# One kernel's expert gelu taken one chunk later, and TensorE's wait moved from the gelu to the sum

## The chip, the cores and the metric

The kernel runs on one core of a Trainium2 chip. The metric is the device time of one execution in microseconds (us). The core's engines work side by side and meet only at semaphores: TensorE (PE; its weight loads are PEld), VectorE (DVE), ScalarE (ACT), GpSimd (POOL) and SyncE (SP), whose queue issues most DMAs.

## The reference

A decoder layer for 256 tokens of width 2048, float32: an input projection, a gated delta rule and a retention beside each other, an output projection, then the part that matters here, and a gated embedding with a last norm. The part that matters is a mixer of 16384 one-neuron experts:

```python
q = (xt @ w_pq).reshape(t, PK_HEADS, 2, PK_DQ // 2)
scores = jnp.einsum('thpc,hpnc->thpn', q, sub_keys)
s1, i1 = lax.top_k(scores[:, :, 0], 16); s2, i2 = lax.top_k(scores[:, :, 1], 16)
# 16 best of the 256 sums per token and head: idx, gates = softmax
pre = jnp.einsum('tkd,td->tk', expert_u[i_blk], x_blk)
act = jax.nn.gelu(pre, approximate=False) * g_blk
out = jnp.einsum('tk,tkd->td', act, expert_v[i_blk])
```

The kernel does not gather. It computes `pre` for all 128 x 128 experts and all tokens, applies the gelu, multiplies by a map of gates that is zero where an expert was not chosen, and multiplies by all of expert_v.

## The kernel before, in words

**Tiles.** All large weights come as one stream of tiles of 128 x 1024 float32 (512 KB). SP loads tile n into one of four `raw` buffers. ScalarE rounds it to `hi` (`round_tile`, L208 to L213), VectorE takes the rest `lo = raw - hi` (`rest_tile`, L215 to L220), TensorE multiplies by both (`pair_tile`, L229 to L242): 8 products of hi with both halves of the activations (512 columns, L236), then 8 of lo with one half (256 columns, L240). There are two `hi` and two `lo` buffers. So round n waits until TensorE is through with hi of tile n-2 (`hi_used`) and VectorE has taken the rest of tile n-2 (`lo_ready`); rest n waits for round n and until TensorE is through with lo of tile n-2 (`lo_used`).

**Expert chunks.** The stage has 128 chunks of 128 experts, two tiles each (T_U on), 256 tiles. Chunk c is accumulated in PSUM bank 6 + c % 2. Its two halves are summed by VectorE into `pre[:, c % 2]` (`take_pre`, L1134 to L1136, one tensor_reduce), which stands in VectorE's queue behind the rest of the second tile of chunk c+1. ScalarE's gelu (`gelu_chunk`, L733 to L735) reads `pre` and writes chunk c to SBUF. In ScalarE's queue the order is: the two rounds of chunk c, then the gelu of chunk c-1 (`expert_round`, L737 to L742). The gelu adds one to `expert_bank`, which starts at 2; TensorE waits for `expert_bank >= c + 1` before chunk c (L1617), that is for the gelu of chunk c-2.

**What VectorE does beside it.** For the first 144 tiles VectorE also chooses the experts. A unit (`choose`, L1138 to L1201) is one head of one block of 128 tokens: eight tiles, and between them the top-16 searches, in an order written out by hand. There are 16 units. After every fourth comes `weigh` (L1211 to L1230): a subtraction of the largest score (L1215, raises `gates_in`), an exp on ScalarE (L751, between expert rounds, it needs another activation table), four plain tiles, and the sums and products of the gates (L1224 to L1230), which raise `gates_ready`. POOL then scatters the gates to a map in HBM, 64 scatters for each `weigh` (L1396). The remaining 112 tiles run without choosing (`plain`, L1203).

**Behind the stage.** SP waits until all 256 scatters have landed (L523), loads the first two blocks of the map (L515), and goes on with the tiles of expert_v. ScalarE's `value_round` (L756) and VectorE's `gated_block` (L1255) begin the next stage; the last gelu and the last sum stand in their first tiles (L768, L1259).

Of the kernel before, what the change touches and what calls it, by code (L numbers as in the profile page):

```python
# [75 lines left out]
CHUNKS = N_KEYS  # L76
# [48 lines left out]
def build(nc, x, w_in_cols, w_in_rows, w_ab, w_out, w_pq, expert_u, expert_v, w_gate, w_ple, p_t,  # L125
          positions, keep_c, mix_c, norm_cols, conv_cols, sub_keys_t, ab_cols, dn_norm, ret_gn_w,
          ret_gn_b, norm_final, out, h_spill, gate_map):
    with ExitStack() as ctx:
# [3 lines left out]
        def sem(name):  # L132
            return ctx.enter_context(nc.semaphore(name))
# [63 lines left out]
        def hold(eng, name, s, value):  # L197

            eng.wait_ge(s, value)
            eng.sem_inc(held[name], 1)  # L200
# [7 lines left out]
        def round_tile(act, n, slot, use, turn, first=False):  # L208
            act.wait_ge(weights_landed[slot], 16 * turn + 16)
            if not first:  # L210
                act.wait_ge(hi_used, n - SPLIT + 1)
                act.wait_ge(lo_ready, n - SPLIT + 1)
            act.activation(hi[:, use, :], raw[:, slot, :], ACT.Copy).then_inc(hi_ready, 1)  # L213
# [8 lines left out]
        def tile_at(base, i, per, k):  # L222

            assert base % RAW == 0 and per % RAW == 0
            return (base + k + per * i, (base + k) % RAW, (base + k) % SPLIT,
                    (base + k) // RAW + (per // RAW) * i)
# [17 lines left out]
        def both_halves(bank):  # L244
            return ps[:, bank, :].rearrange("p (h t) -> p t h", h=2)
# [93 lines left out]
        def wait_turned(pe, turn, d, banks):  # L339
# [93 lines left out]
        expert_bank, gates_in, gates_exp, gates_ready = (sem("expert_bank"), sem("gates_in"), sem("gates_exp"),  # L433
                                                         sem("gates_ready"))
        pre_ready, zeros_ready, map_cleared, gates_placed = sem("pre_ready"), sem("zeros_ready"), sem("map_cleared"), sem("gates_placed")
# [52 lines left out]
        def _(sp):  # L488
# [8 lines left out]
            def stream(base, source, start, stop):  # L497

                with sp.Fori(start, stop) as i:
                    for k in range(RAW):  # L500
                        n, slot, _, _ = tile_at(base, i, RAW, k)
                        load_tile(sp, n, slot, source[ds(i * RAW + k, 1)].rearrange("a p f -> (a p) f"))
# [15 lines left out]
            def value_block(j):  # L518
                for k in range(RAW):
                    n, slot, _, _ = tile_at(T_V, j, RAW, k)  # L520
                    load_tile(sp, n, slot, expert_v[ds(j * RAW + k, 1)].rearrange("a p f -> (a p) f"))
# [21 lines left out]
        def _(act):  # L543
# [189 lines left out]
            def gelu_chunk(c, parity):  # L733
                hold(act, "act", pre_ready, c + 1)
                act.activation(experts[:, ds(c, 1), :], pre[:, parity:parity + 1, :], ACT.Gelu).then_inc(expert_bank, 1)  # L735

            def expert_round(i, first=False):  # L737
                for c in range(2):
                    for k in range(2):
                        round_tile(act, *tile_at(T_U, i, 4, 2 * c + k))  # L740
                    if not (first and c == 0):
                        gelu_chunk(2 * i + c - 1, 1 - c)  # L742

            expert_round(0, first=True)
            for w in range(WEIGHINGS):
                with act.Fori(max(1, WEIGH_ROUNDS * w), WEIGH_ROUNDS * (w + 1) - 1) as i:
                    expert_round(i)

                units = slice(WEIGH_UNITS * w, WEIGH_UNITS * (w + 1))
                act.wait_ge(gates_in, w + 1)  # L750
                act.activation(gates3[:, units], gates3[:, units], ACT.Exp).then_inc(gates_exp, 1)  # L751
                expert_round(WEIGH_ROUNDS * (w + 1) - 1)
# [3 lines left out]
            def value_round(half, i, late=0, first=False):  # L756

                if half == 0:
                    hold(act, "act", gated, i + 1)
                for c in range(4):  # L760
                    v = CHUNKS * half + 4 * i + c
                    if not (first and c < 2):
                        hold(act, "act", lo_used, T_V + v + late - 1)
                    act.activation(stage_hi[:, c % 2:c % 2 + 1, :], experts[:, ds(4 * i + c, 1), :],  # L764
                                   ACT.Copy).then_inc(stage_hi_ready, 1)
                    round_tile(act, T_V + v + late, c % RAW, c % SPLIT, (T_V + late) // RAW + CHUNKS // RAW * half + i)
                    if first and c == 0:
                        gelu_chunk(CHUNKS - 1, 1)  # L768

            value_round(0, 0, first=True)  # L770
            with act.Fori(1, CHUNKS // 4) as i:
                value_round(0, i)
            with act.Fori(0, CHUNKS // 8) as i:
                value_round(1, i)
# [42 lines left out]
        def _(dve):  # L817
# [315 lines left out]

            def take_pre(c, parity):  # L1134
                dve.wait_ge(lo_used, T_U + 2 * c + 2)
                dve.tensor_reduce(pre[:, parity, :], both_halves(U_BANK + parity), AX_X, ALU.add).then_inc(pre_ready, 1)  # L1136

            def choose(w, u):  # L1138
                    unit = WEIGH_UNITS * w + u

                    def tile(k):
                        rest_tile(dve, *tile_at(T_U + WEIGH_TILES * w, u, UNIT_TILES, k)[:3])
                        if k % 2 == 1 and not (w == 0 and isinstance(u, int) and k == 1):
                            take_pre(WEIGH_TILES // 2 * w + UNIT_TILES // 2 * u + (k - 3) // 2, (k - 3) // 2 % 2)
# [58 lines left out]
            def plain(start, stop):  # L1203

                with dve.Fori(start // 2, stop // 2) as i:
                    for k in range(4):
                        rest_tile(dve, *tile_at(T_U, i, 4, k)[:3])
                        if k % 2 == 1:
                            take_pre(2 * i + (k - 3) // 2, (k - 3) // 2 % 2)
# [45 lines left out]
            def gated_block(j, buf, turn, first=False):  # L1255
                for c in range(4):
                    value_tile(0, j, c)
                    if first and c == 0:
                        take_pre(CHUNKS - 1, 1)  # L1259
                    if c == 1:  # L1260
                        apply_gates(j + 1, buf, turn)
# [146 lines left out]
        def _(pe):  # L1408
# [5 lines left out]
            def pair_chunk(base, i, c, turn=None, bank=0):  # L1414
                for k in range(2):
                    n, _, use, _ = tile_at(base, i, 4, 2 * c + k)
                    pair_tile(pe, n, use, k, ps[:, bank + c, :], turn=turn)
# [196 lines left out]

            def expert_round(i):
                for c in range(2):
                    pe.wait_ge(expert_bank, 2 * i + c + 1)  # L1617
                    pair_chunk(T_U, i, c, bank=U_BANK)

            with pe.Fori(0, CHUNKS // 2) as i:  # L1620
                expert_round(i)

            def value_round(half, i, first=False, late=0):
# [110 lines left out]
```

## Time and profile before

| | us |
|---|---|
| three runs, median (lowest to highest) | 2318.5 (2317.56 to 2320.36) |
| the profiled execution | 2315.05 |
| its span in the profile | 2313.2 |
| PE busy in the span | 2198.7 (95%) |
| PEld busy | 1872.2 (81%) |
| DVE busy | 1537.0 (66%) |
| ACT busy | 1057.6 (46%) |
| POOL busy | 493.0 (21%) |

The page cuts the span in 40 slices of 57.8 us. The expert chunks run from about 700 to 1490 us, slices 13 to 26; choosing ends near 1170. Busy time of PE is that of matmuls, whose ends are modelled and which overlap; an engine's idle time is listed with what ended it.

### The profile page before, as it was taken

How to read it: one execution, taken by the hardware profiler on the slowest of the kernel's cores; microseconds unless marked ns; L12 is line 12 of the kernel's file. 1: busy time of each engine (PE TensorE's matmuls, PEld its weight loads, DVE VectorE, ACT ScalarE, POOL GpSimd, SP SyncE). 2: the span in 40 equal slices, each digit the busy share in tenths (PEclk: the TensorE clock that was granted, in tenths of full speed). 3: DMA queues.
4: the chain of work that ended last, by engine and by line, in shares of the span. 5: the costliest groups of instructions: out<-in, count | busy, mean ns of one | idle time of the engine just before them, and what ended most of it. 6: DMA issues, size and time to landing. Idle time of an engine off the chain costs nothing.

```text
span 2313.2 us, 37229 instructions
## 1 busy us (share of the span) xinstructions
PE 2198.7 (95%) x11378; PEld 1872.2 (81%) x11378; DVE 1537.0 (66%) x2247; ACT 1057.6 (46%) x1423; POOL 493.0 (21%) x301
## 2 busy tenths in 40 slices
PE   7999998989999898889899999999999999999997
PEld 7888778978887777777788888888888888888876
DVE  6885777865546777777755555666666666566565
ACT  6543664234433333434344444444554555445554
POOL 0112000200000068777777760000000000000000
PEclk9999997999999999999999999999999999999999
DMA  5765567035554466666677775676766655656544
GB/s 196 239 192 164 180 202 279 0 120 196 184 173 137 154 164 158 160 162 156 163 182 189 190 184 190 218 240 239 246 237 240 213 190 192 230 191 196 193 163 145
DMA packets 157117, 430.86 MB, mean 186 GB/s; under 512 B 49552, under 2 KB 49936, under 8 KB 155408
## 3 DMA queue, kind: packets, MB, share of 16 engines
q1 hardware_dynamic: 118080, 417.59, 54.3%
q0 software_dynamic: 36864, 0.15, 4.4%
q10 hardware_dynamic: 2128, 12.58, 1.5%
q8 instruction: 21, 0.34, 0.1%
q14 instruction: 24, 0.20, 0.0%
HBM read 409.15 MB, written 21.10 MB: 186 GB/s over the span
## 4 chain that ended last, share of the span: by engine, by line
PE 75%; DVE 9%; DVEq 6%; ACT 4%; issue 3%; DMA 1%; ACTq 0%; SPq 0%
PE ps L1632 20%; PE ps L236 18%; PE ps L1639 10%; PE ps L240 9%; PE ps L261 5%; PE ps L255 4%; PE ps L256 4%; ACT hi L213 3%; DVE lo L219 3%; DVEq L1158 2%; PE ps L320 1%; PE ps L1540 1%; DVEq L1165 1%; PE ps L1547 1%; DVE arena L1152 1%
## 5 line engine op out<-in xcount | busy, mean ns | idle before, releaser
L219 DVE TENSOR_TENSOR lo<-raw,hi 128x1024 fp32r<-128x1024 f32 x724 | 892.5, 1236 | 509.4 <-ACT hi L213 493.1
L213 ACT ACTIVATE hi<-raw 128x1024 fp32r<-128x1024 f32 x724 | 755.0, 1052 | 346.3 <-PE ps L236 181.9
L236 PE MATMUL ps<-act_pair,hi 128*128 128x512 f32 x2816 | 715.2, 396 | 52.3 <-ACT hi L213 52.1
L236 PEld LDWEIGHTS ps<-act_pair,hi 128*128 128x128 f32 x2816 | 506.6, 189 | 157.2 <-ACT hi L213 65.5
L1396 POOL DMA_INDIRECT gate_map<-gate_in_sb x256 | 432.8, 1691 | 507.7 <-DVEq L1230 380.2
L240 PEld LDWEIGHTS ps<-act_pair,lo 128*128 128x128 f32 x2816 | 383.5, 191 | 35.3 <-DVE lo L219 8.3
L240 PE MATMUL ps<-act_pair,lo 128*128 128x256 f32 x2816 | 394.9, 283 | 2.3 <-DVE lo L219 2.3
L1632 PE MATMUL ps<-hi,stage_hi 128*128 128x512 f32 x1024 | 274.1, 389 | 0.6 <-ACT hi L213 0.5
L1632 PE MATMUL ps<-hi,stage_lo 128*128 128x512 f32 x1024 | 273.7, 389 | 0.0
L1639 PE MATMUL ps<-lo,stage_hi 128*128 128x512 f32 x1024 | 273.7, 389 | 0.0
L764 ACT ACTIVATE stage_hi<-arena 128x256 fp32r (+1 forms) x256 | 106.9, 418 | 341.4 <-PE ps L1639 338.8
L735 ACT ACTIVATE arena<-pre 128x256 f32 (+1 forms) x128 | 53.4, 418 | 388.9 <-DVE pre L1136 388.8
L1632 PEld LDWEIGHTS ps<-hi,stage_hi 128*128 128x128 f32 x1024 | 191.8, 188 | 41.7 <-issue 1.2
L1632 PEld LDWEIGHTS ps<-hi,stage_lo 128*128 128x128 f32 x1024 | 192.2, 188 | 40.0
L1639 PEld LDWEIGHTS ps<-lo,stage_hi 128*128 128x128 f32 x1024 | 192.2, 188 | 39.9
L1404 POOL TENSOR_TENSOR arena<-arena 128x1024 f32<-128x1024 f32 x3 | 7.2, 2396 | 904.0 <-DVE arena L1319 904.0
L1251 DVE TENSOR_TENSOR stage_lo<-arena,stage_hi 128x256 fp32r<-128x256 f32 x256 | 108.8, 425 | 134.2 <-ACT stage_hi L764 134.2
L255 PE MATMUL ps<-hi,act_pair 128*128 128x512 f32 x464 | 184.2, 397 | 0.3 <-DVE act_pair L336 0.3
L256 PE MATMUL ps<-hi,act_pair 128*128 128x512 f32 x464 | 180.8, 390 | 0.0
L261 PE MATMUL ps<-lo,act_pair 128*128 128x512 f32 x464 | 125.2, 392 | 1.4 <-DVE lo L219 1.4
L261 PEld LDWEIGHTS ps<-lo,act_pair 128*128 128x128 f32 x464 | 86.5, 188 | 21.9 <-DVE lo L219 4.1
L255 PEld LDWEIGHTS ps<-hi,act_pair 128*128 128x128 f32 x464 | 87.1, 188 | 20.4 <-issue 2.4
(226 smaller groups left out, 1286.7 us busy)
## 6 DMA issues: line engine op xcount, KB each, us to landing
raw<-in_expert_u SPq DMA_DIRECT2D x256, 512.0 KB, 3.3
raw<-in_expert_v SPq DMA_DIRECT2D x256, 512.0 KB, 3.3
raw<-in_w_in_cols SPq DMA_DIRECT2D x64, 512.0 KB, 3.3
raw<-in_w_in_rows SPq DMA_DIRECT2D x48, 512.0 KB, 3.3
gate_map<-stage_lo SPq DMA_DIRECT2D x1, 16384.0 KB, 47.3
raw<-in_w_out SPq DMA_DIRECT2D x32, 512.0 KB, 3.3
raw<-in_w_pq SPq DMA_DIRECT2D x32, 512.0 KB, 3.3
gate_in_sb<-gate_map SPq DMA_DIRECT2D x32, 512.0 KB, 4.2
```

The costliest lines, as they stand in the source:

```text
L213: act.activation(hi[:, use, :], raw[:, slot, :], ACT.Copy).then_inc(hi_ready, 1)
L219: dve.tensor_tensor(lo[:, use, :], raw[:, slot, :], hi[:, use, :].bitcast(F32), ALU.subtract).then_inc(lo_ready, 1)
L236: mm = pe.matmul(out_ap, hi[:, use, d8 * P:(d8 + 1) * P], act_pair[:, d, :], start=(d == 0), stop=False)
L240: mm = pe.matmul(out_ap[:, 0:SEQ], lo[:, use, d8 * P:(d8 + 1) * P], act_hi[:, 8 * k + d8, :], start=False, stop=(k == 1 and d8 == 7))
L255: pe.matmul(outs[tb], act_hi[:, d, t], w, start=(d == 0), stop=False)
L256: mm = pe.matmul(outs[tb], act_lo[:, d, t], w, start=False, stop=False)
L261: mm = pe.matmul(outs[tb], act_hi[:, 2 * k + k2, tb * P:tb * P + P], lo[:, use, k2 * 512:(k2 + 1) * 512], start=False, stop=(k == last and ...
L764: act.activation(stage_hi[:, c % 2:c % 2 + 1, :], experts[:, ds(4 * i + c, 1), :], ACT.Copy).then_inc(stage_hi_ready, 1)
L1251: dve.tensor_tensor(stage_lo[:, c % 2:c % 2 + 1, :], experts[:, ds(4 * i + c, 1), :], stage_hi[:, c % 2:c % 2 + 1, :].bitcast(F32), ALU.su ...
L1396: pool.indirect_dma_start(gate_map, bass.IndirectOffsetOnAxis(ap=place[:, unit, r:r + 1], axis=0), gates_out[:, unit, r:r + 1], None, comp ...
L1632: mm = pe.matmul(ps[:, 4 * half + 2 * tb + b, :], a[:, use, tb * P:(tb + 1) * P], hi[:, use, b * 512:(b + 1) * 512], start=(first and c == ...
L1639: mm = pe.matmul(ps[:, 4 * half + 2 * tb + b, :], stage_hi[:, use, tb * P:(tb + 1) * P], lo[:, use, b * 512:(b + 1) * 512], start=False, s ...
```

## The change

ScalarE makes the gelu of chunk c-2 behind the rounds of chunk c (it was that of chunk c-1), and the last two gelus fall into the first two value tiles. TensorE waits, before chunk c from chunk 2 on, for VectorE's sum of chunk c-2 (`pre_ready >= c - 1`). VectorE waits, before it sums chunk c, for the gelu of chunk c-2, which reads the same half of `pre`.

```diff
                 for c in range(2):
                     for k in range(2):
                         round_tile(act, *tile_at(T_U, i, 4, 2 * c + k))
-                    if not (first and c == 0):
-                        gelu_chunk(2 * i + c - 1, 1 - c)
+                    if not first:
+                        gelu_chunk(2 * i + c - 2, c)
...
-                    if first and c == 0:
-                        gelu_chunk(CHUNKS - 1, 1)
+                    if first and c < 2:
+                        gelu_chunk(CHUNKS - 2 + c, c)
...
             def take_pre(c, parity):
                 dve.wait_ge(lo_used, T_U + 2 * c + 2)
+                dve.wait_ge(expert_bank, c + 1)
                 dve.tensor_reduce(pre[:, parity, :], both_halves(U_BANK + parity), AX_X, ALU.add).then_inc(pre_ready, 1)
...
             def expert_round(i):
                 for c in range(2):
-                    pe.wait_ge(expert_bank, 2 * i + c + 1)
+                    if not (isinstance(i, int) and i == 0):
+                        pe.wait_ge(pre_ready, 2 * i + c - 1)
                     pair_chunk(T_U, i, c, bank=U_BANK)
 
-            with pe.Fori(0, CHUNKS // 2) as i:
+            pe.wait_ge(expert_bank, 2)
+            expert_round(0)
+            with pe.Fori(1, CHUNKS // 2) as i:
                 expert_round(i)
```

## Rows read from the trace of the kernel before

**Rows 1.** Busy time of each engine (instructions) in two stretches; then clock, DMA share, GB/s.

```profile
705.00:1170.00 465.00, 415.00 (x2260) 350.56 (x2260) 350.23 (x818) 178.95 (x224) 277.07 (x159) 1.00 0.62 159
...
1200.00:1400.00 200.00, 200.00 (x1146) 175.93 (x1145) 109.11 (x107) 89.20 (x108) 132.62 (x84) 1.00 0.76 187
```

**Rows 2.** Who waited for whom, 705 to 1170: us, times, longest.

```profile
ACT arena L735 <- DVE pre L1136: 266.8, 65, 4.7
...
PEld ps L236 <- ACT hi L213: 62.6, 62, 2.4
```

**Rows 3.** Timeline of weight loads, two stretches: start, length, engine, line.

```profile
968.64 1.01 PEld L240 LDWEIGHTS ps<-act_pair,lo 128*128 128x128 f32 x8 [0.30 <-DVE lo L219]
...
1202.84 1.70 PEld L236 LDWEIGHTS ps<-act_pair,hi 128*128 128x128 f32 x8
1204.57 1.13 PEld L240 LDWEIGHTS ps<-act_pair,lo 128*128 128x128 f32 x8
...
1208.42 1.70 PEld L236 LDWEIGHTS ps<-act_pair,hi 128*128 128x128 f32 x8
```

**Rows 4.** Timeline of VectorE in one unit: its rests and last sum; in brackets idle before.

```profile
963.93 1.23 DVE L219 TENSOR_TENSOR lo<-raw,hi 128x1024 fp32r<-128x1024 f32 x1 [1.85 <-ACT hi L213]
...
967.37 1.22 DVE L219 TENSOR_TENSOR lo<-raw,hi 128x1024 fp32r<-128x1024 f32 x1 [0.23 <-issue]
...
970.79 1.23 DVE L219 TENSOR_TENSOR lo<-raw,hi 128x1024 fp32r<-128x1024 f32 x1 [0.51 <-ACT hi L213]
...
977.70 1.23 DVE L219 TENSOR_TENSOR lo<-raw,hi 128x1024 fp32r<-128x1024 f32 x1 [0.85 <-ACT hi L213]
...
980.31 1.23 DVE L219 TENSOR_TENSOR lo<-raw,hi 128x1024 fp32r<-128x1024 f32 x1 [0.21 <-issue]
...
983.73 1.23 DVE L219 TENSOR_TENSOR lo<-raw,hi 128x1024 fp32r<-128x1024 f32 x1 [1.00 <-ACT hi L213]
...
986.70 1.23 DVE L219 TENSOR_TENSOR lo<-raw,hi 128x1024 fp32r<-128x1024 f32 x1 [0.22 <-issue]
987.84 0.68 DVE L1136 TENSOR_REDUCE pre<-ps 128x256 f32<-128x512 f32 x1
990.38 1.23 DVE L219 TENSOR_TENSOR lo<-raw,hi 128x1024 fp32r<-128x1024 f32 x1 [1.85 <-ACT hi L213]
```

**Rows 5.** Timeline of ScalarE behind that sum.

```profile
988.72 0.42 ACT L735 ACTIVATE arena<-pre 128x256 f32 x1 [4.07 <-DVE pre L1136]
989.20 2.01 ACT L213 ACTIVATE hi<-raw 128x1024 fp32r<-128x1024 f32 x2
```

**Rows 6.** Timeline of VectorE: the first and the last of four gates subtractions.

```profile
805.22 0.22 DVE L1215 TENSOR_TENSOR arena<-arena 128x64 f32<-128x64 f32 x1
...
1160.30 0.22 DVE L1215 TENSOR_TENSOR arena<-arena 128x64 f32<-128x64 f32 x1
```

**Rows 7.** Timeline of VectorE: rests on either side of the second exp.

```profile
922.15 1.23 DVE L219 TENSOR_TENSOR lo<-raw,hi 128x1024 fp32r<-128x1024 f32 x1 [0.21 <-issue]
...
927.14 1.22 DVE L219 TENSOR_TENSOR lo<-raw,hi 128x1024 fp32r<-128x1024 f32 x1 [2.30 <-ACT hi L213]
```

**Rows 8.** Timeline of ScalarE at that exp.

```profile
924.61 1.28 ACT L751 ACT_TABLE_LOAD   x1
925.90 0.26 ACT L751 ACTIVATE arena<-arena 128x64 f32<-128x64 f32 x1
```

**Rows 9.** Timeline of VectorE: rest 0 and rest 31 of the stage.

```profile
700.55 1.23 DVE L219 TENSOR_TENSOR lo<-raw,hi 128x1024 fp32r<-128x1024 f32 x1 [9.43 <-ACT hi L213]
...
803.48 1.23 DVE L219 TENSOR_TENSOR lo<-raw,hi 128x1024 fp32r<-128x1024 f32 x1 [0.22 <-issue]
```

**Rows 10.** The line of the sum's first wait: ns min/median/max, first and last start.

```profile
L1135 DVEq FUSED_REGOPS  x116: 53/65/75, 730.3 to 1482.6; - x116
```

**Rows 11.** The gate map: its scatters by line, and SP's first loads of it.

```profile
L1396 POOL DMA_INDIRECT gate_map<-gate_in_sb x256: 1544/1547/2602, 818.9 to 1377.6; - x128
...
1473.40 0.83 SPq L515 DMA_DIRECT2D gate_in_sb<-gate_map  x2
```

## Prediction

> **What bounds the kernel now.** I read the windows first, because the change touches one stage only, the 128 expert chunks. In the windows [rows 1] the reader is to see two halves of that stage. From 1200 to 1400 us TensorE's matmuls are busy without a gap and VectorE 55%. From 705 to 1170 us, where VectorE also chooses experts (16 units of 8 tiles, a gate group of 4 tiles after every fourth unit), TensorE is busy 415.0 of 465 us and VectorE 350.2. The granted clock is 1.00 in both, 2.4 GHz, the upper of its two levels, so neither half is slowed by it. Second view, the waits of that first half [rows 2]: ScalarE's gelu waited 266.8 us for VectorE's sum, and TensorE's weight loads waited 62.6 us for ScalarE's rounded tile. So the kernel is bound by TensorE behind 1170 us, and in front of it by a ring through three engines.
>
> How fast is TensorE when nothing holds it? The weight loads of the second half [rows 3] begin a tile's hi part at 1202.84, its lo part 1.73 later, and the next chunk at 1208.42: 5.58 us a chunk, 2.79 a tile (1.73 hi, 1.06 lo).
>
> The ring is in the timelines of one unit. VectorE [rows 4] starts its eight rests (L219) from 963.93 to 986.70 and the next unit's first at 990.38: 26.45 us, where TensorE alone would need 8 x 2.79 = 22.32. (Seven of the eight are in the rows; the one left out is like that at 980.31.) Four waited for ScalarE: 0.51, 0.85, 1.00, 1.85, together 4.21 us. The last shows why: rest at 986.70, sum (L1136) at 987.84, on ScalarE [rows 5] gelu at 988.72, round at 989.20, next rest at 990.38. From the sum's start that is 0.88 to the gelu, 0.48 more to the round (with a loop's branch), 1.18 more to the rest: 2.54 us in which VectorE had 0.68 us of its own work. ScalarE could have rounded that tile long before; the gelu stood in front of it in its queue.
>
> The Trainium skill ("Perfetto Trace Analysis", Identifying the Most-Contended Engine) says that matmul busy time misleads as a measure of headroom and that weight-load busy time is better. The trace agrees: by matmuls 50 of 465 us are free [rows 1], while weight loads are busy 350.6 of 465, 0.754, against 175.9 of 200, 0.880, where nothing waits. By that ratio some 66 us of the 465 are lost; by matmul gaps the most to be had would be 50.
>
> **The change, part by part.**
> (a) ScalarE order. Before: round 2c, round 2c+1, gelu c-1. After: the same two rounds, then gelu c-2. That sum was made behind rest 2c-1, which round 2c+1 needs anyway (two hi buffers), so at the gelu's place it is there: the sum ends 1.14 + 0.68 us behind the start of rest 2c-1 [rows 4], while round 2c+1 can't begin before that rest ends and takes another 1.05. Round 2c+2 now waits only for TensorE's hi part of tile 2c and the rest of it. TensorE issues a hi part in 1.73 us; for its last product and the hand-over I take 0.4 (no row has it alone; between 0 and the 1.06 of the lo part behind it). The round with its hand-over takes at most the 1.18 of [rows 4, 5]. So the tile is ready 3.3 us (2.9 to 4.0) behind the hi part two tiles earlier; it is wanted at 5.58. The 4.21 us of ScalarE waits per unit go.
>
> (b) What is late next: VectorE itself. Of each of the four waits about 0.21 is not wait but the issue that rests without a wait show too (0.21 to 0.23 [rows 4]). So a unit costs VectorE 26.45 - 4.21 + 4 x 0.21 = 23.08 us, against TensorE's 22.32. VectorE becomes the bound inside the units by a little; two buffers let it be late by less than 3 us without TensorE noticing, but each gate group takes the slack back, as follows.
>
> (c) A gate group stays a stop. ScalarE's exp waits for gates_in, which VectorE raises after the sum behind the unit's last rest, and the next tile's round is queued behind the exp. Before, rest to rest over this place is 922.15 to 927.14, 4.99 us [rows 7]. After, the gelu is not in it: the subtraction of gates starts at +1.74 (803.48 to 805.22 [rows 6, 9]) and takes 0.22, the hand-over to ScalarE 0.20 (as from sum to gelu: 987.84 + 0.68 to 988.72 gives 0.20 [rows 4, 5]), then 1.29 from table load to exp [rows 8] and 1.24 from exp to rest [rows 7, 8]: 4.7 us. Then TensorE is first again: the rest four tiles on can start when the lo part two tiles before it ends, 3 x 2.79 + 0.4 = 8.8 us later. The gelu table comes back behind the group's second round (1.28 + 0.42 us on ScalarE), where TensorE has two tiles, 5.58 us, in front of the hi part of the next round: hidden.
>
> (d) Sum from one gates subtraction to the next (36 tiles). Before: from 805.22 to 1160.30 are three such intervals [rows 6], 118.36 each. After: 4.7 + 8.8 + four units less the last segment (4 x 23.08 - 2.04 = 90.3, where 2.04 is 990.38 - 986.70 - 1.85 + 0.21) = 103.8. Gain 14.56, three times 43.7. The first four units, rest 0 to rest 31, took 700.55 to 803.48 = 102.9 us [rows 9]; after, 90.3 less one sum (0.6, the first half chunk has none) = 89.7, gain 13.2. The last exp gives 0.3. Sum 57.2.
>
> (e) VectorE's new wait for expert_bank ahead of each sum. Queued behind it are the rest of choosing and the next rest, for which TensorE waits. Gelu c-2 is in ScalarE's queue ahead of round 2c+2, and the sum of c stands behind rest 2c+3, so the count is always reached. Its issue: the register step on the sum's line takes 65 ns [rows 10], a second one and a semaphore step would be about 0.1. The cover is the rest in front: the sum starts 1.14 us after the rest starts, before that rest's 1.23 us are over [rows 4], with the existing register step already inside. Bounds: 0, or 0.1 to 0.2 exposed on some 66 sums, 6.6 to 13. I take 0, as the rows of hidden steps are nearest.
>
> (f) TensorE's wait for pre_ready instead of expert_bank: same number of register steps. The sum of c-2 is ready 1.14 + 0.68 + 0.1 (an estimate, half of the 0.20 above) = 1.9 us after rest 2c-1 starts; TensorE takes the lo part of that tile 1.27 after the start at the earliest (967.37 to 968.64 [rows 3, 4]) and needs 1.06 for it, so it asks at 2.33. Margin 0.4 us where VectorE is the bound, more elsewhere. Cost 0.
>
> (g) Second half (from 1170 us): TensorE has no gap there [rows 1], so rounds that come earlier gain nothing: 0. The two gelus of the last chunks move into the first value tiles, 0.42 us each behind rounds, on an engine 45% busy there: 0, at worst 1 us.
>
> (h) SP's queue: it waits for all 256 scatters before it loads the first gate maps at 1473.40; the last scatter starts at 1377.6 [rows 11]. The stage ends about 57 us sooner, at about 1416 for these loads. The scatters start when the first gates are ready, 13 us sooner, and the four batches of 64 follow one another at POOL's own pace: about 1365. 50 us spare, cost 0.
>
> I take 1.2 off the 57.2 for holds on VectorE that the chosen unit doesn't show: 56 us. Against the profiled execution's own 2315.05 (span 2313.2) that is 2259. The median of the runs is 2318.5, 3.45 above it, so I forecast 2262.
>
> **Rivals.**
> A. VectorE keeps up and TensorE is the bound everywhere. For: 23.08 and 22.32 are close. Against: gate groups give the lead back. Interval 36 x 2.79 = 100.4, gain 17.9 x 3 = 53.8; first stretch 31 x 2.79 = 86.5, gain 16.4; 70.6 in all: 2248.
> B. More of VectorE's path is exposed: the new wait (6.6 to 13 us), or a floor of a unit 5% larger. For: I see its floor only through waits. 2269 to 2276.
> C. The change does not take the wait away: VectorE waits as long for the round, which now waits for TensorE's hi part (two buffers). For: behind 1170 us VectorE is idle 45% of the time and the ring is as slow as TensorE. Against: 3.2 against 5.58 us in (a). About 2318.
> D. Slower: TensorE stands at every chunk for the sum, the 0.4 us margin of (f) being negative. Place: between tile 2c-1 and 2c. A sum late by x costs x - 0.4 per chunk in the 70 chunks of the first half; it eats the 56 us from x = 1.2 and costs more than 0.2% from x = 1.3; at x = 1.5 the time is 2318 + 77 - 56 = 2339. For: the sum is behind VectorE's longest queue. Against: it stands directly behind the rest that TensorE also needs.
> E. The scatters end too late. The Trainium skill ("SBUF — State Buffer", Who interferes with whom) says that VectorE operations with two SBUF inputs and GpSimd's lock each other out of a shared port, so a denser VectorE would stretch the scatters. What it would take by the rows: the 559 us of scatters would have to become 10% longer to end at 1421, 5 us behind the 1416 of (h); the time would then be 2267, and each us beyond is one of the kernel.
>
> **How the numbers follow.** Forecast 0.60 (2257 to 2267); A 0.14; B 0.18; C 0.04; D 0.03; E 0.01. The range takes in A and B: 2249 to 2279. A change of 0.2%, 4.6 us, is what a measurement of this kernel can tell from none. Faster 0.93, same 0.04, slower 0.03.
>
> **What would show it.** In the changed kernel: the gelu's wait for the sum gone or nearly; rests in the units without waits for ScalarE but 0.21 to 0.23 us of issue; a unit of about 23.1 us; gates subtractions 104 us apart; the exp group with TensorE waiting about 2 us, four times; 1200 to 1400's pace (5.58 a chunk) unchanged; everything behind shifted by 56 us. A unit of 22.3 would mean A, sums that start later than 1.14 us behind the rest B, waits of L219 for ScalarE C, TensorE waiting on L1136 D, and SP idle before the map loads E. The forecast is wrong if the intervals are longer than 107 or shorter than 101 us.

## The result and the profile after

The changed kernel takes 2291.86 us, median of four runs (2284.8, 2285.74, 2297.98, 2300.99), against 2319.43 before (2317.56 to 2320.4). The ratio is 0.9888, 95% interval 0.987 to 0.9905: 26 us faster by the ratio (27.6 between the two medians), where 56 were forecast, and outside the range of 2249 to 2279. The profiled execution took 2284.8 us, span 2283.0, 30 us less than before. The runs of the changed kernel also lie 16 us apart, those before 3.

The stage itself is much as forecast. First the windows (busy us of PE, PEld, DVE, ACT, POOL with counts; clock, DMA share, GB/s), to be held against [rows 1]:

```profile
705.00:1107.00 402.00, 398.48 (x2260) 344.89 (x2259) 350.92 (x815) 200.27 (x238) 243.89 (x131) 1.00 0.67 184
1120.00:1410.00 290.00, 290.00 (x1664) 255.24 (x1663) 158.18 (x157) 126.08 (x156) 240.46 (x104) 1.00 0.66 188
```

TensorE does the same 2260 matmuls in 402 us that took 465, with 3.5 us of gaps instead of 50. VectorE's second unit behind the second exp (timeline: five of its eight rests, then the next unit's first at 948.34; against [rows 4]):

```profile
925.18 1.22 DVE L219 TENSOR_TENSOR lo<-raw,hi 128x1024 fp32r<-128x1024 f32 x1
...
928.61 1.24 DVE L219 TENSOR_TENSOR lo<-raw,hi 128x1024 fp32r<-128x1024 f32 x1 [0.23 <-issue]
...
931.76 1.23 DVE L219 TENSOR_TENSOR lo<-raw,hi 128x1024 fp32r<-128x1024 f32 x1 [0.21 <-issue]
...
938.03 1.22 DVE L219 TENSOR_TENSOR lo<-raw,hi 128x1024 fp32r<-128x1024 f32 x1 [0.21 <-ACT hi L213]
...
943.52 1.23 DVE L219 TENSOR_TENSOR lo<-raw,hi 128x1024 fp32r<-128x1024 f32 x1 [0.21 <-PE ps L240]
...
948.34 1.22 DVE L219 TENSOR_TENSOR lo<-raw,hi 128x1024 fp32r<-128x1024 f32 x1
```

That is 23.16 us for this unit. The steady ones, the second and third behind each exp, take 22.8 to 23.2. No idle is left in front of these rests but 0.21 to 0.23 us of issue; rests that waited for nothing show the same 0.21, so the engine named behind such a 0.21 held nothing up. Next the gates subtractions (against [rows 6]) with VectorE's rests around the second exp (against [rows 7]), and then ScalarE at that exp (against [rows 8]):

```profile
788.20 0.22 DVE L1216 TENSOR_TENSOR arena<-arena 128x64 f32<-128x64 f32 x1
...
889.61 1.25 DVE L219 TENSOR_TENSOR lo<-raw,hi 128x1024 fp32r<-128x1024 f32 x1 [0.21 <-issue]
...
891.38 0.21 DVE L1216 TENSOR_TENSOR arena<-arena 128x64 f32<-128x64 f32 x1
892.86 1.23 DVE L219 TENSOR_TENSOR lo<-raw,hi 128x1024 fp32r<-128x1024 f32 x1 [0.34 <-ACT hi L213]
...
1097.32 0.21 DVE L1216 TENSOR_TENSOR arena<-arena 128x64 f32<-128x64 f32 x1
```

```profile
886.93 1.28 ACT L751 ACT_TABLE_LOAD   x1
891.62 0.26 ACT L751 ACTIVATE arena<-arena 128x64 f32<-128x64 f32 x1 [3.41 <-issue]
```

Three intervals between gates subtractions are 309.1 us, 103.04 each. From rest to rest over the exp it is 3.25 us. Then the page's line on the chain of work that ended last, and the waits around the end of the stage (engine, line, what it waited for: us, times, longest; the last line is SP's own queue):

```profile
POOL gate_map L1397 21%; PE ps L1636 20%; PE ps L1643 10%; PE ps L236 10%; PE ps L240 5%; PE ps L261 5%; PE ps L255 5%; PE ps L256 5%; DMA gate_map<-gate_in_sb 3%; PE ps L320 1%; PE ps L1548 1%; PE ps L1550 1%; PE ps L1541 1%; PE ps L1491 1%; DVE lo L219 0%
```

```profile
ACT stage_hi L764 <- DVE arena L1244: 34.5, 1, 34.5
...
PE ps L1636 <- ACT hi L213: 32.8, 1, 32.8
DVE arena L1244 <- DMA gate_in_sb<-gate_map: 31.6, 1, 31.6
...
SPq L515 <- DMA gate_map<-gate_in_sb: 39.2, 1, 39.2
```

Before, POOL did not stand in the chain's line; now its scatters are 21% of the span. TensorE waits 32.8 us once, at the first expert_v tile. The waits name ScalarE, but ScalarE waits for VectorE, VectorE for the load of the gates' map, and SP, which issues that load, waits 39.2 us for the scatters to land. Now the scatters by line (ns min/median/max, first and last start), then SP's last expert_u tiles and its first map loads, against [rows 11]:

```profile
L1397 POOL DMA_INDIRECT gate_map<-gate_in_sb x256: 1544/2252/2610, 799.3 to 1444.7; - x128
```

```profile
1396.75 11.51 SPq L206 DMA_DIRECT2D raw<-in_expert_u  x5
1447.60 0.82 SPq L515 DMA_DIRECT2D gate_in_sb<-gate_map  x2
```

The 256 scatters took 645 us from first to last start, not 559, with a median of 2.25 us instead of 1.55. They end 67 us later than before. Why one is longer is in the timelines of POOL and of VectorE behind choosing (start, length; in brackets idle before):

```profile
1300.62 2.49 POOL L1397 DMA_INDIRECT gate_map<-gate_in_sb  x1 [0.30 <-issue]
1303.41 2.40 POOL L1397 DMA_INDIRECT gate_map<-gate_in_sb  x1 [0.30 <-issue]
1306.12 2.49 POOL L1397 DMA_INDIRECT gate_map<-gate_in_sb  x1 [0.30 <-issue]
```

```profile
1300.46 1.23 DVE L219 TENSOR_TENSOR lo<-raw,hi 128x1024 fp32r<-128x1024 f32 x1 [1.57 <-ACT hi L213]
...
1303.17 1.23 DVE L219 TENSOR_TENSOR lo<-raw,hi 128x1024 fp32r<-128x1024 f32 x1 [0.88 <-ACT hi L213]
1305.96 1.23 DVE L219 TENSOR_TENSOR lo<-raw,hi 128x1024 fp32r<-128x1024 f32 x1 [1.57 <-ACT hi L213]
```

Each scatter starts 0.16 to 0.24 us behind the start of a rest and is some 0.9 us longer; the next one starts 0.30 behind its end, which is again just behind the start of the next rest, since the rests now come evenly, 2.7 to 2.9 us apart. Before, the gelu in the ring made them come in pairs, 2.0 to 2.1 and 3.4 to 3.7 us apart, and the scatters ran through at one in 1.85 us (kernel before, POOL, then VectorE):

```profile
1303.17 1.55 POOL L1396 DMA_INDIRECT gate_map<-gate_in_sb  x1 [0.31 <-issue]
1305.02 1.55 POOL L1396 DMA_INDIRECT gate_map<-gate_in_sb  x1 [0.30 <-issue]
1306.87 1.55 POOL L1396 DMA_INDIRECT gate_map<-gate_in_sb  x1 [0.30 <-issue]
```

```profile
1301.79 1.23 DVE L219 TENSOR_TENSOR lo<-raw,hi 128x1024 fp32r<-128x1024 f32 x1 [1.60 <-ACT hi L213]
1303.86 1.23 DVE L219 TENSOR_TENSOR lo<-raw,hi 128x1024 fp32r<-128x1024 f32 x1 [0.84 <-ACT hi L213]
...
1307.55 1.23 DVE L219 TENSOR_TENSOR lo<-raw,hi 128x1024 fp32r<-128x1024 f32 x1 [1.87 <-ACT hi L213]
1309.53 1.22 DVE L219 TENSOR_TENSOR lo<-raw,hi 128x1024 fp32r<-128x1024 f32 x1 [0.76 <-ACT hi L213]
```

The changed kernel's own trace shows the other side too. Its last rest of the stage starts at 1417.70, and from 1420.65 on every scatter takes 1.55 us again (that rest, then POOL):

```profile
1417.70 1.23 DVE L219 TENSOR_TENSOR lo<-raw,hi 128x1024 fp32r<-128x1024 f32 x1 [1.57 <-ACT hi L213]
```

```profile
1418.57 1.77 POOL L1397 DMA_INDIRECT gate_map<-gate_in_sb  x1 [0.30 <-issue]
1420.65 1.55 POOL L1397 DMA_INDIRECT gate_map<-gate_in_sb  x1 [0.30 <-issue]
...
1444.71 1.55 POOL L1397 DMA_INDIRECT gate_map<-gate_in_sb  x1 [0.30 <-issue]
```

The first of these starts 0.87 us behind that rest's start and ends 2.64 behind it. This is a rule of all the traces whose rests have both inputs in SBUF (the two kernels and all the experiments below but e4): between 1200 and 1416 us, 302 scatters start 0.05 to 1.05 us behind a rest's start, and every one ends 2.64 to 2.66 us behind that start; the 348 that start more than 1.15 us behind it take 1.54 to 1.56 us.

### The profile page after: what moved, and what is told of

The parts are those of the page before. It is cut to its first block, busy times and chain, and to the rows that moved or that the text cites. A ratio compares the mean times of both kernels' runs of the same rounds, so it can differ in the third digit from the quotient of the medians.

```text
span 2283.0 us, 37241 instructions
## 1 busy us (share of the span) xinstructions
PE 2184.4 (96%) x11378; PEld 1869.3 (82%) x11378; DVE 1537.1 (67%) x2247; ACT 1075.5 (47%) x1436; POOL 585.2 (26%) x301
## 4 chain that ended last, share of the span: by engine, by line
PE 65%; POOL 21%; issue 5%; DMA 4%; DVE 3%; DVEq 1%; ACT 1%; SPq 0%; ACTq 0%; POOLq 0%
POOL gate_map L1397 21%; PE ps L1636 20%; PE ps L1643 10%; PE ps L236 10%; PE ps L240 5%; PE ps L261 5%; PE ps L255 5%; PE ps L256 5%; DMA gate_map<-gate_in_sb 3%; PE ps L320 1%; PE ps L1548 1%; PE ps L1550 1%; PE ps L1541 1%; PE ps L1491 1%; DVE lo L219 0%
## 5 line engine op out<-in xcount | busy, mean ns | idle before, releaser
L213 ACT ACTIVATE hi<-raw 128x1024 fp32r<-128x1024 f32 x724 | 763.0, 1055 | 650.2 <-PE ps L236 462.1
L236 PE MATMUL ps<-act_pair,hi 128*128 128x512 f32 x2816 | 707.3, 393 | 4.5 <-ACT hi L213 4.5
L1397 POOL DMA_INDIRECT gate_map<-gate_in_sb x256 | 525.3, 2052 | 484.5 <-DVEq L1231 362.9
L1636 PE MATMUL ps<-hi,stage_hi 128*128 128x512 f32 x1024 | 274.9, 390 | 32.9 <-ACT hi L213 32.8
L255 PEld LDWEIGHTS ps<-hi,act_pair 128*128 128x128 f32 x464 | 87.1, 188 | 20.4 <-issue 2.5
L256 PEld LDWEIGHTS ps<-hi,act_pair 128*128 128x128 f32 x464 | 87.1, 188 | 19.8 <-issue 1.9
```

The costliest lines, as they stand in the source:

```text
L236: mm = pe.matmul(out_ap, hi[:, use, d8 * P:(d8 + 1) * P], act_pair[:, d, :], start=(d == 0), stop=False)
L255: pe.matmul(outs[tb], act_hi[:, d, t], w, start=(d == 0), stop=False)
L256: mm = pe.matmul(outs[tb], act_lo[:, d, t], w, start=False, stop=False)
L1397: pool.indirect_dma_start(gate_map, bass.IndirectOffsetOnAxis(ap=place[:, unit, r:r + 1], axis=0), gates_out[:, unit, r:r + 1], None, comp ...
L1636: mm = pe.matmul(ps[:, 4 * half + 2 * tb + b, :], a[:, use, tb * P:(tb + 1) * P], hi[:, use, b * 512:(b + 1) * 512], start=(first and c == ...
```

## Experiments

All edits are against the changed kernel. "Batch" is the time from the first to the last start of the 64 scatters of one `weigh`. The changed kernel has 145, 148, 174 and 164 us, the kernel before 140, 138, 136 and 130. Chunk 72 is where choosing ends.

**e1, the old order where no experts are chosen.** From chunk 72 on, ScalarE's gelus go back to their old place.

```diff
+            def old_round(i, first=False):
+                for c in range(2):
+                    for k in range(2):
+                        round_tile(act, *tile_at(T_U, i, 4, 2 * c + k))
+                    if first and c == 0:
+                        gelu_chunk(2 * i - 2, 0)
+                    gelu_chunk(2 * i + c - 1, 1 - c)
...
-            with act.Fori(WEIGHINGS * WEIGH_ROUNDS, CHUNKS // 2) as i:
-                expert_round(i)
+            old_round(WEIGHINGS * WEIGH_ROUNDS, first=True)
+            with act.Fori(WEIGHINGS * WEIGH_ROUNDS + 1, CHUNKS // 2) as i:
+                old_round(i)
...
-                    if first and c < 2:
-                        gelu_chunk(CHUNKS - 2 + c, c)
+                    if first and c == 0:
+                        gelu_chunk(CHUNKS - 1, 1)
```

> The changed kernel, but from chunk 72 on (no choosing any more) ScalarE's gelus go back to their old place; TensorE's and VectorE's new waits stay. My theory: the change won some 62 us in the first half and lost 35 behind it, because with the gelu late VectorE's rests come evenly, 2.79 us apart, each scatter of GpSimd then starts just behind the start of a rest and takes 2.4 to 2.5 us instead of 1.55, and SP waits for the last of 256 scatters. With the old order behind, the rests come in pairs again (about 2.0 and 3.6 us apart), batches 3 and 4 of the scatters take 130 to 140 us instead of 174 and 164, the last scatter starts near 1380, before SP asks at about 1416, and the 33 us wait goes: 2247 to 2255 us, with a spread below 4 us between runs. Rival (the scatters became slow because the stage in front is denser, or because DMA queues are fuller, not by the spacing of rests): batch 3 and 4 still near 165 to 174 us and the time 2280 to 2300.

Measured: 2252.89 us (2250.3 to 2253.71, five runs), ratio to the kernel before 0.9715 (0.9701 to 0.9728). Batches 3 and 4 took 134 and 130 us. Scatters, and SP's first map load:

```profile
L1406 POOL DMA_INDIRECT gate_map<-gate_in_sb x256: 1545/1548/2592, 801.2 to 1372.4; - x128
L515 SPq DMA_DIRECT2D gate_in_sb<-gate_map x32: 332/332/425, 1410.4 to 1739.1; - x32
```

The last scatter starts 38 us before SP asks. So the loss is undone by the order of the second half alone, and this version beats both kernels: 65 us below the one before.

**e2, three batches.** The gates of the last four units are left out of the map.

```diff
-            for w in range(WEIGHINGS):
+            for w in range(WEIGHINGS - 1):
                 pool.wait_ge(gates_ready, w + 1)
...
-            sp.wait_ge(gates_placed, 16 * 16 * TOPK)
+            sp.wait_ge(gates_placed, 16 * 12 * TOPK)
```

> The changed kernel without the fourth batch of scatters, and SP waits for 192 of 256 (this leaves the gates of the last four units out of the map). If the end of the scatters sets the start of the next stage and nothing else was lost: the 33 us wait goes, and with it a slow clock behind it, 2247 to 2253 us, and the spread of 16 us between runs of the changed kernel falls below 4. Rival (the next stage waits for something else, the first loads of the map or the two gelus that moved into its tiles): TensorE's wait stays above 10 us and the time above 2260.

Measured: 2250.21 us (2250.11 to 2251.23, four runs), ratio 0.9706 (0.9692 to 0.9721), though its third batch took 185 us. SP's first map load:

```profile
L515 SPq DMA_DIRECT2D gate_in_sb<-gate_map x32: 332/333/424, 1409.4 to 1737.7; - x32
```

The scatters' end is the whole loss: in the profiled executions the spans are 2248.5 against 2283.0, 34.5 us, of which 32.8 are TensorE's wait, and the medians are 42 us apart. The runs now lie 1.1 us apart, so the spread came from the scatters too. e2 has the late gelus everywhere, and the last two in the next stage's first tiles, and is 2.7 us below e1; it also has a quarter of the scatters less, but e8 below, which has them all, is not above e1 either. The moved gelus cost nothing that shows.

**e3, the waits alone.** ScalarE's gelus stay where they were before; TensorE and VectorE have the new waits.

```diff
-                    if not first:
-                        gelu_chunk(2 * i + c - 2, c)
+                    if not (first and c == 0):
+                        gelu_chunk(2 * i + c - 1, 1 - c)
...
-                    if first and c < 2:
-                        gelu_chunk(CHUNKS - 2 + c, c)
+                    if first and c == 0:
+                        gelu_chunk(CHUNKS - 1, 1)
```

> Only the waits of the change (TensorE for VectorE's sum, VectorE for the gelu two chunks back), with ScalarE's gelus where they were before. If the wait that counted was ScalarE's, for the sum in front of its next round: no change, 2315 to 2322 us. If TensorE's release from the gelu was what won the time: below 2300. If the added wait costs VectorE issue time of 0.1 us a sum, some 6 us more than before: 2324.

Measured: 2319.19 us (2316.51 to 2320.07, ten runs), ratio 1.0001 (0.9992 to 1.0011). TensorE's release from the gelu wins nothing by itself; the time is won only with ScalarE's new order. Whether that order would win it with TensorE's old wait, no run shows. The waits cost nothing measurable here, where VectorE still has idle time in the units; that they cost nothing in the changed kernel either is seen in its trace, where the sums still start 1.13 to 1.17 us behind the rest in front, as before.

**e4, a rest with one input from SBUF.** Behind chunk 72 the rest is raw minus a pair of PSUM banks that is idle in this stage, so the low parts of these tiles are not the reference's.

```diff
+        def rest_from_psum(dve, n, slot, use):
+            dve.wait_ge(hi_ready, n + 1)
+            dve.wait_ge(lo_used, n - SPLIT + 1)
+            dve.tensor_tensor(lo[:, use, :], raw[:, slot, :], ps[:, 0:2, :].rearrange("p b c -> p (b c)"),
+                              ALU.subtract).then_inc(lo_ready, 1)
...
-            plain(WEIGHINGS * WEIGH_TILES // 2, CHUNKS)
+            plain(WEIGHINGS * WEIGH_TILES // 2, CHUNKS, rest_from_psum)
```

> The changed kernel, but behind chunk 72 the rest is taken as raw minus a PSUM bank pair instead of raw minus hi (same size, one input from SBUF instead of two; the low parts of these tiles are not those of the reference). If a scatter is held up by a VectorE operation that reads two inputs from SBUF: scatters in batches 3 and 4 go back to 1.55 us each and 1.85 apart, about 125 to 130 us a batch, though the rests stay 2.8 us apart; time 2247 to 2256. If it is held up by something else in that rhythm (TensorE's or ScalarE's traffic, the weight DMAs): scatters stay 2.79 apart, the time 2280 to 2300. The duration of this form of the rest is open, 1.1 to 1.3 us.

Measured: 2250.62 us (two runs), ratio 0.9707 (0.9689 to 0.9725); batches 3 and 4 took 131 and 126 us. VectorE's timeline, then the scatters from 1180 to 1360 us by line (count, busy us, mean ns), first of this kernel and then of the changed one:

```profile
1301.48 1.22 DVE L225 TENSOR_TENSOR lo<-raw,ps 128x1024 fp32r<-128x1024 f32 x1 [1.57 <-ACT hi L213]
...
1304.19 1.22 DVE L225 TENSOR_TENSOR lo<-raw,ps 128x1024 fp32r<-128x1024 f32 x1 [0.88 <-ACT hi L213]
1306.98 1.22 DVE L225 TENSOR_TENSOR lo<-raw,ps 128x1024 fp32r<-128x1024 f32 x1 [1.57 <-ACT hi L213]
```

```profile
L1403 POOL DMA_INDIRECT gate_map<-gate_in_sb x89 | 137.7, 1547 | 44.2 <-issue 31.0 <-DMA gate_map<-gate_in_sb 13.2
```

```profile
L1397 POOL DMA_INDIRECT gate_map<-gate_in_sb x65 | 152.9, 2352 | 31.4 <-issue 20.9 <-DMA gate_map<-gate_in_sb 10.5
```

The rests have the same length and the same rhythm, and no scatter is held up: mean 1.547 us, 89 of them where there were 65. Of the scatters between 1180 and 1400 us, 66 of 78 in the changed kernel start within 0.9 us behind a rest's start, with a median of 2.49 us; here 30 of 90 do, and the longest of these is 1.55. So it is VectorE's second read from SBUF that holds a scatter up. The Trainium skill ("SBUF — State Buffer", Who interferes with whom) says that a VectorE instruction with two SBUF inputs contends with a GpSimd instruction that reads SBUF. The traces agree, if a scatter counts as one: it takes its 128 offsets and its 128 values from SBUF. The same section of the Trainium skill infers that such a VectorE instruction does not stall GpSimd's descriptor generation for a DMA. These scatters are held up all the same; whether at the read of the offsets or at the descriptors, no run here shows.

**e5, the late gelu only where no experts are chosen.** The mirror of e1: before chunk 72 ScalarE has the old order, from there on the new one (`new_round`).

```diff
-                    if not first:
-                        gelu_chunk(2 * i + c - 2, c)
+                    if not (first and c == 0):
+                        gelu_chunk(2 * i + c - 1, 1 - c)
+
+            def new_round(i, first=False):
+                for c in range(2):
+                    for k in range(2):
+                        round_tile(act, *tile_at(T_U, i, 4, 2 * c + k))
+                    if not (first and c == 0):
+                        gelu_chunk(2 * i + c - 2, c)
...
-            with act.Fori(WEIGHINGS * WEIGH_ROUNDS, CHUNKS // 2) as i:
-                expert_round(i)
+            new_round(WEIGHINGS * WEIGH_ROUNDS, first=True)
+            with act.Fori(WEIGHINGS * WEIGH_ROUNDS + 1, CHUNKS // 2) as i:
+                new_round(i)
```

> The mirror of e1: ScalarE's gelus in their old place while experts are chosen, in the new place from chunk 72 on. My theory: nothing is won in the first half, and behind it the rests come evenly, so scatter batches 3 and 4 (136 and 130 us in the kernel before) take 160 to 185 us; the last scatter starts at 1430 to 1470 instead of 1378. SP asks at about 1473, so that costs nothing or a few us: 2316 to 2326 us. Rival (the late gelu as such wins something behind 1170 us too): below 2310. Rival (scatters are slow only where the stage in front was shortened): batches stay 130 to 137 us.

Measured: 2317.38 us, ratio 0.9999 (0.9989 to 1.0009), batches 3 and 4 156 and 176 us; scatters from 1180 to 1360 us:

```profile
L1405 POOL DMA_INDIRECT gate_map<-gate_in_sb x63 | 148.7, 2361 | 31.3 <-issue 20.4 <-DMA gate_map<-gate_in_sb 10.9
```

From 1180 to 1360 us they are as slow as in the changed kernel (mean 2.36 and 2.35 us) without anything shortened in front of them. The last one starts at 1443, 32 us before SP asks at 1475, so it costs nothing. The late gelu wins nothing behind the choosing.

**e6 and e8, rounds in pairs with the gelu late.** Both add one wait ahead of the two rounds of a chunk from chunk 72 on; e6 for the rest of the tile before, e8 for the sum of chunk c-2 (each kernel has one of the two waits shown).

```diff
+            def paired_round(i):
+                for c in range(2):
+                    act.wait_ge(pre_ready, 2 * i + c - 1)          # e8
+                    act.wait_ge(lo_ready, T_U + 4 * i + 2 * c)     # e6
+                    for k in range(2):
+                        round_tile(act, *tile_at(T_U, i, 4, 2 * c + k))
+                    gelu_chunk(2 * i + c - 2, c)
...
             with act.Fori(WEIGHINGS * WEIGH_ROUNDS, CHUNKS // 2) as i:
-                expert_round(i)
+                paired_round(i)
```

> The changed kernel with the gelus late everywhere, but from chunk 72 on ScalarE waits with the first round of a chunk until the rest of the tile before it is taken, so that rounds and rests come nearer to pairs while the gelu stays late. If the spacing of the rests is what slows the scatters: gaps of the rests no longer all 2.7 to 2.9 us, batches 3 and 4 clearly below 174 and 164 us (130 to 145 if the pairs are as in the kernel before), 2248 to 2260 us. If it is the gelu's place in itself: batches above 160 us, 2280 to 2300 us. The wait may turn out to change nothing, if the rest is always taken by then; the gaps of the rests show which of the two it is.

> The changed kernel with the gelus late everywhere, but from chunk 72 on ScalarE waits, ahead of the two rounds of chunk c, for the sum of chunk c-2 (the wait that e6 put there was met already). So rounds and rests must come in pairs while the gelu stays late. If the spacing of the rests slows the scatters: gaps of the rests alternate, about 2.0 and 3.6 us, batches 3 and 4 take 130 to 145 us, 2247 to 2258 us. If the gelu's place in itself does: batches above 160 us, 2280 to 2310 us.

e6: 2289.26 us, five runs from 2281.8 to 2308.86, ratio 0.9884 (0.9842 to 0.9927), as the changed kernel. The rests are still 2.65 to 2.84 us apart, and in the timeline the rounds start when TensorE is through with `hi`: the rest was taken by then, so the run says nothing of pairs. It does show the spread. In its profiled execution, of 2306.18 us, batches 3 and 4 took 186 and 163 us and TensorE waited 52.9 us, 20 more than in the profiled execution of the changed kernel, with nearly the same rhythm of rests.

e8: 2251.45 us (2250.39 to 2253.01, four runs), ratio 0.9711 (0.9695 to 0.9727), batches 133 and 129 us. The spacing is 2.4 us and 3.1 or 3.3 in turn, less uneven than expected, but enough:

```profile
1301.31 1.23 DVE L219 TENSOR_TENSOR lo<-raw,hi 128x1024 fp32r<-128x1024 f32 x1 [1.18 <-ACT hi L213]
...
1304.40 1.23 DVE L219 TENSOR_TENSOR lo<-raw,hi 128x1024 fp32r<-128x1024 f32 x1 [1.26 <-ACT hi L213]
1306.81 1.23 DVE L219 TENSOR_TENSOR lo<-raw,hi 128x1024 fp32r<-128x1024 f32 x1 [1.19 <-ACT hi L213]
```

It is the spacing of the rests, not the place of the gelu.

Why 2.9 us is too little and 3.1 enough can be worked out from the rows above. This is an estimate. A scatter that is held up ends 2.65 us behind the rest's start, and the next one starts 0.30 later, at 2.95. If the next rest has begun by then, the next scatter is held up too, and so on: the scatters are locked to the rests. If a gap between rests is longer than 2.95, the next scatter starts ahead of the rest and gets free. Between 1200 and 1400 us the changed kernel, e2, e5 and e6, whose scatters are held up, have no gap above 2.88; the kernel before, e1, e3, e7 and e8, whose scatters run through, have one of 3.08 or more in every chunk.

**e7, more work for VectorE.** e1 with the first copy of each unit made four times, a drain behind each.

```diff
                     dve.tensor_copy(key_in, scores[:, ds(unit, 1)].rearrange("p a k n -> p (a k) n"))
+                    dve.drain()
+                    dve.tensor_copy(key_in, scores[:, ds(unit, 1)].rearrange("p a k n -> p (a k) n"))
...
```

> e1 with VectorE's first copy of each unit made four times instead of once, with a drain behind each (three more copies and drains, some 0.4 us each, about 1.2 us a unit, 16 units, the output is the same). If VectorE is the bound within the units since the change, as step (b) of the prediction has it, nearly all of it shows: 14 to 20 us more than e1, 2267 to 2273 us. If TensorE is the bound and VectorE has slack (rival A): less than 4 us more, below 2257.

Measured: 2272.46 us (2271.99 to 2273.09, four runs), ratio to the kernel before 0.9799 (0.9783 to 0.9815). That is 19.6 us above e1, 1.22 us for each of 16 units. A unit grows from 23.1 us to 24.3 in the steady ones. In VectorE's timeline the added work is 1.30 us (first copy to first search: 0.36 us in e1, 1.66 in e7), so nearly all of it shows: within the units VectorE is the bound.

## Why the prediction was wrong

**Right: the ring, (a).** Nearly all waits for ScalarE in the units are gone, and by e3 the new waits without ScalarE's order win nothing.

**Right: VectorE as the next bound, (b) and (d).** The unit was forecast at 23.08 us and is 23.16 where shown; the interval was forecast at 103.8 and is 103.04; e7 shows that the bound is VectorE. The first stretch, rest 0 to rest 31, went from 102.9 to 88.3 us (698.16 to 786.45; 89.7 forecast). From its first rest (698.2) to its last (1417.7) the stage takes 719.5 us instead of 782.1 (700.6 to 1482.6): 62.6 us less, where 57.2 were worked out and 56 forecast.

**Missed by size: the stop at the exp, (c).** I put the table load behind gates_in, 4.7 us from rest to rest. It is 3.25: with the gelu made early, ScalarE is idle there and loads the table at 886.93, while only the exp waits, until 891.62. TensorE's records show 0.75 us of idle time at that place, not the 2 forecast (2.10 before). Four times 1.45 is 5.8 us. The first stretch, which has no exp in it, won another 1.4, and the rest of the stage gave 1.8 back: together the 5.4 us beyond the sum.

**Right: the new waits, (e) and (f).** They cost nothing in e3, the sums of the changed kernel start no later behind their rests, and TensorE is never seen waiting for a sum.

**Wrong: (h), the step that failed.** It said that the scatters "follow one another at POOL's own pace: about 1365" and put their cost at 0. POOL's pace hangs on VectorE's rhythm: 559 us became 645, the last scatter started at 1444.7 instead of 1365, and SP, which would have asked at 1409 as in e2, issued its load at 1447.6. That is some 38 us late, of which 32.8 reached TensorE, and 34.5 the span. Without this term the forecast would have been 12 us too high (e2, 2250.21 against 2262); with it the kernel takes 42 us more than e2 in the median. So the error of 30 is the difference of two. Rival E had the place, its sign (SP idle before the map loads) came true, and its price, 2267 at 1421 and each us beyond one more, gives 2291 at 1444.7; that this is nearly the median measured is in part luck, since it starts from the 2262 that was 12 too high. But its chance was 0.01, the stretch of 10% that it took to matter was a number I had not tested against any row, and its reason, a denser VectorE, is not the one. What decides is not how busy VectorE is (55% in both kernels, from 1200 us in [rows 1], from 1120 here) but where in a rest a scatter begins, and the change alters just that: it takes the gelu, which made the rests uneven, out of the ring. I had counted the moved gelus behind 1170 us as 0 because TensorE is the bound there, step (g), and did not ask who else runs beside the rests. e1, e4, e5 and e8 settle it.

**A slip in rival B.** Its floor of a unit 5% larger would cost 16 x 1.15 = 18 us, 2280 and not 2276. Nothing measured hangs on it.

**Open.** Why the executions of the changed kernel and of e6 differ among themselves by 16 and 27 us: e2 shows that the scatters are the reason, and scatters that lock to the rests may lock earlier or later, but only one execution of each has a profile. Why batches 1 and 2, beside the denser units, take 145 and 148 us instead of 140 and 138. Whether the late gelu with TensorE's old wait would do as well.

## What to carry to other kernels

When a stage gets shorter, list every queue that has to be done by its end, and its spare time. Here 50 us of spare were used up because one scatter in 1.85 us became one in 2.79 through half of the stage. An edit that is free for the bounding engine still changes the rhythm of the others: look for an engine that shares something with one whose instructions move, and compare start against start in the timeline, not busy shares. Make the change only where it wins: the late gelu in the half that was bound by the ring, the old order behind it, is 65 us faster than before, the change everywhere 26.

## What the runs showed of the hardware

- The engines do not meet only at semaphores. A scatter (indirect DMA of GpSimd, 128 elements) takes 1.55 us, but one that begins up to 1.05 us behind the start of a VectorE operation of 1.23 us with two SBUF inputs ends 2.64 to 2.66 us behind that start (302 scatters), which makes it up to 2.6 us long. With one of the inputs in PSUM it is 1.55 wherever it begins (e4, 30 scatters within 0.9 us).
- Such a scatter stream can lock to VectorE's rhythm: one in 2.79 us at 2.79 a tile, where one in 1.85 is possible. It did so where no gap between rests was above 2.88 us, and not where every second one was 3.1 or more.
- An activation table load is not held by the wait of the activation behind it: its 1.28 us are hidden in the changed kernel, where ScalarE had been idle (load at 886.93, exp at 891.62), and exposed in the kernel before, where the gelu came just in front (load at 924.61, exp at 925.90).
- TensorE's clock fell while it stood still in the 32.8 us wait: granted 1.00, that is 2.4 GHz, from 1400 to 1423 us, 0.50, that is 1.2 GHz, from 1430 to 1456, and 0.69 on the mean from 1456 to 1462, when the matmuls had begun again. Those 6 us at a mean of 0.69 cost, as an estimate, some 1.9 us. The windows of the changed kernel:

```profile
1450.00:1456.00 6.00, 0.06 (x1) 0.07 (x1) 1.73 (x3) 1.59 (x3) 0.00 (x0) 0.50 0.98 347
...
1456.00:1462.00 6.00, 6.00 (x19) 4.82 (x20) 4.77 (x6) 3.04 (x6) 0.00 (x0) 0.69 0.94 353
```
